# Last quad of the down projection by token halves, a stacked operand for the time steps, and a later sum of squares in a hybrid decoder layer on one Trainium2 core

## What is computed

```python
def rmsnorm(x, g):
    y = x * lax.rsqrt(jnp.mean(x * x, axis=-1, keepdims=True) + EPS)
    return y * g
...
dt = softplus(h @ w_in[:, dt_columns] + ssm_dt_bias)      # 16 heads
h_t = exp(dt_t * A) * h_{t-1} + dt_t * x_t * B_t^T ;  y_t = h_t @ C_t + D * x_t
ssm = rmsnorm(y * silu(z), ssm_norm_g) @ ssm_w_out
...
x3 = x2 + ffn @ ffn_w_down
y  = rmsnorm(x3, final_norm_g)
```

## Time and profile before

| | |
|---|---|
| median of 3 runs | 1029.4 us (1029.18 to 1032.2) |
| profiled execution | 1031.21 us, of it 1029.4 us span |
| TensorE matmul busy | 1002.2 us (97%), 7994 instructions |
| VectorE busy | 623.4 us (61%) |
| ScalarE busy | 381.2 us (37%) |
| GpSimd busy | 282.0 us (27%) |
| granted TensorE clock, mean | 0.988 of full |

### The profile page before, as it was taken

How to read it: one execution, slowest core, us unless ns; L and a number is a source line. 1 busy time by engine, 2 the same in 40 slices (tenths; PEclk the granted TensorE clock), 3 DMA queues, 4 the chain that set the end, 5 groups by cost and what they waited for, 6 DMA issues and landing times.

```text
span 1029.4 us, 19474 instructions
## 1 busy us (share of the span) xinstructions
PE 1002.2 (97%) x7994; PEld 980.2 (95%) x7994; DVE 623.4 (61%) x970; ACT 381.2 (37%) x544; POOL 282.0 (27%) x212
## 2 busy tenths in 40 slices
PE   5999999999999999999999999999999999999996
PEld 5999989989998999989999999999999999999996
DVE  4799879975547788796533335555540036666453
ACT  4322337653631665525222334433321122322210
POOL 3200000000030001452344334444434454444350
PEclk9999989999999999999999999999999999999997
DMA  7423227323322323415272222323223332321222
GB/s 237 147 83 99 65 62 63 66 63 92 89 73 62 104 83 117 171 41 185 82 248 85 83 86 80 93 92 99 64 62 93 100 110 89 99 66 53 76 59 87
DMA packets 42605, 97.96 MB, mean 95 GB/s; under 512 B 14640, under 2 KB 15536, under 8 KB 42544
## 3 DMA queue, kind: packets, MB, share of 16 engines
q1 hardware_dynamic: 42544, 97.10, 31.8%
HBM read 89.15 MB, written 7.93 MB: 94 GB/s over the span
## 4 chain that ended last, share of the span: by engine, by line
PE 86%; DVE 11%; issue 1%; POOL 1%; ACT 1%; DMA 0%; SPq 0%; DVEq 0%
PE accs L382 79%; DVE temps L1480 2%; DVE ca L1417 2%; DVE w_split L330 1%; PE misc L950 1%; PE misc L1112 1%; PE misc L956 1%; DVE part L444 1%; PE misc L1077 1%; PE misc L963 1%; PE misc L1128 1%; POOL w_split L330 1%; PE misc L1117 1%; PE misc L1096 1%; DVE xbc L2078 0%
## 5 line engine op out<-in xcount | busy, mean ns | idle before, releaser
L382 PE MATMUL accs<-h_split,w_split 128*128 128x272 f32 x4992 | 637.1, 289 | 4.6 <-POOL h_split L580 2.9
L382 PEld LDWEIGHTS accs<-h_split,w_split 128*128 128x128 f32 x4992 | 628.9, 189 | 10.2 <-issue 4.4
L330 POOL TENSOR_TENSOR w_split<-w_raw,w_split 128x1024 fp32r<-128x1024 f32 (+2 forms) x112 | 252.6, 2263 | 445.1 <-ACT w_split L325 422.3
L382 PE MATMUL accs<-branch,w_split 128*128 128x272 f32 x2208 | 284.8, 290 | 0.0
L382 PEld LDWEIGHTS accs<-branch,w_split 128*128 128x128 f32 x2208 | 280.2, 189 | 3.0 <-issue 2.8
L325 ACT ACTIVATE w_split<-w_raw 128x1024 fp32r<-128x1024 f32 (+3 forms) x168 | 160.0, 962 | 238.4 <-PE accs L382 238.2
L1417 DVE SCALAR_TENSOR_TENSOR ca<-part,params,ca 128x512 f32<-128x512 f32 x120 | 83.7, 749 | 0.4
L330 DVE TENSOR_TENSOR w_split<-w_raw,w_split 128x1024 fp32r<-128x1024 f32 (+1 forms) x56 | 62.1, 1109 | 29.0 <-ACT w_split L325 28.8
L2066 DVE TENSOR_TENSOR xbc<-accs,xbc 128x544 f32<-128x544 f32 x16 | 11.6, 725 | 95.6 <-PE accs L382 95.6
L2043 DVE TENSOR_TENSOR temps<-temps,mixed 128x512 f32<-128x512 f32 x22 | 40.7, 1850 | 26.5 <-ACT temps L920 26.5
L768 ACT ACTIVATE temps<-accs,params 128x544 f32<-128x544 f32 x24 | 17.2, 715 | 93.1 <-PE accs L382 93.1
(11 more groups left out here) (253 smaller groups left out, 710.8 us busy)
## 6 DMA issues: line engine op xcount, KB each, us to landing
w_raw<-in_ffn_w_up SPq DMA_DIRECT2D x44, 512.0 KB, 3.6
w_raw<-in_w_in_main SPq DMA_DIRECT2D x28, 512.0 KB, 3.6
w_raw<-in_w_gate SPq DMA_DIRECT2D x24, 512.0 KB, 3.7
w_raw<-in_ffn_w_down SPq DMA_DIRECT2D x16, 384.0 KB, 3.0
w_raw<-in_ffn_w_down SPq DMA_DIRECT2D x16, 320.0 KB, 2.9
xbc<-in_x SPq DMA_DIRECT2D x16, 272.0 KB, 5.7
w_raw<-in_w_in_z SPq DMA_DIRECT2D x8, 512.0 KB, 3.5
w_raw<-in_ssm_w_out SPq DMA_DIRECT2D x8, 512.0 KB, 3.6
```

The costliest lines, as they stand in the source:

```text
L330: e.tensor_tensor(w_split[:, s, 1, 0:n], w_raw[:, s, 0:n], w_split[:, s, 0, 0:n].bitcast(F32), ALU.subtract).then_inc(w_lo[s], 1)
L382: mm = pe.matmul(accs[:, a, half, 0:HALF], w_split[:, s, wp, k * P:(k + 1) * P], rhs(s, k, xp, half), start=(first and k == 0 and n == 0), ...
```

## The change

Three edits in the work and one in bookkeeping.

1. **End.** D2's last quad runs all four slots for the left 272 tokens and then all four for the right ones. VectorE adds, squares and sums each half of blocks 6 and 7 by itself; each half has its own `token_sum`, root, reciprocal and `spread_rms` of three columns. The left half's `token_sum` stands inside the right half's stream before slot 1, its `spread_rms` in slot 2 at k-tile 1. The eight blocks are scaled and stored by halves (16 stores of 128 x 272).
2. **Time steps.** High and low weight parts lie side by side as 32 weight columns, so that one matmul over 272 columns makes both products: 32 matmuls. Five fp32 matmuls against a matrix `fold_dt` (32 x 16) add the two parts and turn them; `fold_dt` is one more small load on SyncE's queue. ScalarE copies 272 and 272 columns from 32 partitions.
3. **Sum of squares of the gated SSD.** `token_sum` moves from k = 2 to k = 4 of slot 1, `spread_rms` from k = 7 of slot 1 to k = 0 of slot 2. `new_state(3)` moves ahead of `y_times_z(6)`.
4. Five semaphores of cleared buffers become one that counts.

```diff
+            sp.dma_start(fold_dt[:, :], ins["fold_dt"]).then_inc(sem("small_landed"), 16)
...
-            for j in range(KD):
-                sp.wait_ge(sem("y_done"), j + 1)
-                sp.dma_start(outs["y"][:, j], xbc[:, j]).then_inc(sem("stored_y"), 16)
+            for n, (half, j) in enumerate(halves_out):
+                sp.wait_ge(sem("y_done"), n + 1)
+                sp.dma_start(outs["y"][:, j, tokens(half)], xbc[:, j, tokens(half)]).then_inc(sem("stored_y"), 16)
...
-                    act.activation(dt_rows[:, 0:SEQ], misc[0:HEADS, 2], ACT.Copy)
-                    act.activation(dt_rows[:, SEQ:TOK], misc[0:HEADS, 1, 0:SMP], ACT.Copy).then_inc(sem("dt_rows"), 1)
+                    act.activation(dt_rows[:, 0:HALF], misc[0:2 * HEADS, 2, 0:HALF], ACT.Copy)
+                    act.activation(dt_rows[:, HALF:TOK], misc[0:2 * HEADS, 1, 0:HALF], ACT.Copy).then_inc(sem("dt_rows"), 1)
...
-            act_phase(act, "D2", lambda i, s: None)
+            p = ph["D2"]
+            loop(act, 0, p.quads - 1, lambda i: act_quad(act, p, i, (p, i + 1), lambda i, s: None))
             sqrt_table()
-            root("nf", D)
+            for half in range(2):
+                c = slice(3 * half, 3 * half + 3)
+                act.wait_ge(sem("rms_sum"), nth("nf") + half)
+                act.activation(rms[:, 0, c], misc[:, 3, c], ACT.Sqrt, bias=eps[:, 0:1], scale=1.0 / D)\
+                    .then_inc(sem("rms_root"), 1)
...
-                    pe.transpose(misc[:, 2, c * HEADS:(c + 1) * HEADS], dt_rows[:, c * CH:(c + 1) * CH],
-                                 ident[0:HEADS, 0:HEADS])
+                    pe.matmul(misc[:, 2, c * HEADS:(c + 1) * HEADS], dt_rows[:, c * CH:(c + 1) * CH], fold_dt[:, :],
+                              start=True, stop=True)
...
-                    for n, (wp, xp) in enumerate(((0, 0), (0, 1), (1, 0))):
-                        for bank, cols in ((2, slice(0, SEQ)), (1, slice(SEQ, TOK))):
-                            mm = pe.matmul(misc[0:HEADS, bank, 0:cols.stop - cols.start], w_dt_split[:, wp, k],
-                                           h_split[:, k, xp, cols],
-                                           start=(k == 0 and n == 0), stop=(k == KD - 1 and n == 2))
+                    for half in range(2):
+                        for xp in range(2):
+                            mm = pe.matmul(misc[0:2 * HEADS, 2 - half, 0:HALF],
+                                           w_dt_split[:, k].rearrange("p q h -> p (q h)"), h_rhs(0, k, xp, half),
+                                           start=(k == 0 and xp == 0), stop=(k == KD - 1 and xp == 1))
...
-                if (s, k) == (1, 2):
+                if (s, k) == (1, 4):
                     pe.wait_ge(sem("yz_sq"), 1)
                     token_sum(T(2))
-                if (s, k) == (1, 7):
+                if (s, k) == (2, 0):
                     spread_rms("ns")
...
+            def last_halves():
+
+                i = p.quads - 1
+                for half in range(2):
+                    for s in range(SLOTS):
+                        a = p.acc(s)
+                        if half == 0:
+                            pe.wait_ge(w_lo[s], i + (p.quad0 + 1))
+                            if s % 2 == 0:
+                                pe.wait_ge(acc_free[a], p.pair(i, s))
+                        for k in range(p.kb[s]):
+                            if (half, s, k) == (1, 1, 0):
+                                pe.wait_ge(sem("x3_sq"), 1)
+                                token_sum(T(5), range(3))
+                            if (half, s, k) == (1, 2, 1):
+                                spread_rms("nf", range(3))
+                            for n, (wp, xp) in enumerate(((0, 0), (0, 1), (1, 0))):
+                                mm = pe.matmul(accs[:, a, half, 0:HALF], w_split[:, s, wp, k * P:(k + 1) * P],
+                                               rhs(s, k, xp, half), start=(s % 2 == 0 and k == 0 and n == 0),
+                                               stop=(s % 2 == 1 and k == p.kb[s] - 1 and n == 2))
+                        if s % 2:
+                            mm.then_inc(sem("last_half"), 1)
+            last_halves()
             keep_warm(WARM[3])
-            pe.wait_ge(sem("x3_sq"), 1)
-            token_sum(T(5))
+            pe.wait_ge(sem("x3_sq"), 2)
+            token_sum(T(5), range(3, 6))
             keep_warm(WARM[1])
-            spread_rms("nf")
+            spread_rms("nf", range(3, 6), 1)
...
             for k in range(KD):
+                if k == 6:
+                    new_state(3)
                 y_times_z(k)
...
                 if k == 6:
-                    for q in (3, 4, 5):
+                    for q in (4, 5):
                         new_state(q)
...
-            down("D2", True)
-            rstd("nf")
-            for j in range(KD):
-                dve.scalar_tensor_tensor(out=halves(xbc[:, j]), in0=halves(xbc[:, j]), scalar=param("final_g", j),
-                                         in1=stat, op0=ALU.mult, op1=ALU.mult).then_inc(sem("y_done"), 1)
+            down("D2", True, KD - 2)
+            def last_block(half, j):
+                a, own = j % 2, xbc[:, j, tokens(half)]
+                dve.wait_ge(sem("last_half"), 2 * half + a + 1)
+                link(dve.tensor_tensor(own, accs[:, a, half, 0:HALF], own, ALU.add))
+                link(dve.tensor_tensor(T(4)[:, tokens(half)], own, own, ALU.mult))
+                sums = T(5)[:, tokens(half)]
+                if j < KD - 1:
+                    link(dve.tensor_tensor(sums, sums, T(4)[:, tokens(half)], ALU.add))
+                else:
+                    dve.tensor_tensor(sums, sums, T(4)[:, tokens(half)], ALU.add).then_inc(sem("x3_sq"), 1)
+            def inverse_half(half):
+                c = slice(3 * half, 3 * half + 3)
+                dve.wait_ge(sem("rms_root"), nth("nf") + half)
+                dve.reciprocal(rms[:, 1, c], rms[:, 0, c]).then_inc(sem("rms_inverse"), 1)
+            def scaled_half(half, js):
+                dve.wait_ge(sem("rms_spread"), nth("nf") + half)
+                for j in js:
+                    own = xbc[:, j, tokens(half)]
+                    dve.scalar_tensor_tensor(out=own, in0=own, scalar=param("final_g", j), in1=misc[:, half, 0:HALF],
+                                             op0=ALU.mult, op1=ALU.mult).then_inc(sem("y_done"), 1)
+            last_block(0, KD - 2)
+            last_block(0, KD - 1)
+            inverse_half(0)
+            last_block(1, KD - 2)
+            scaled_half(0, range(6))
+            last_block(1, KD - 1)
+            scaled_half(0, range(6, KD))
+            inverse_half(1)
+            scaled_half(1, range(KD))
```

More of the change, by code:

```diff
@@ L37 @@
 EPS = 1e-6
+EPS_SET, ROWS_ZERO, ZEROS_A, ZEROS_X, ZEROS_F = range(1, 6)
 SLOTS = 4
@@ L169, in build @@
         fold = sb("fold", [P, SMP])
+        fold_dt = sb("fold_dt", [2 * HEADS, HEADS])
         head_of = sb("head_of", [64, HEADS], F32R)
@@ L239, in head_decay @@
             return T(2 + h % 4, SEQ)
-        dt_rows = temps[0:HEADS, 5, 0:TOK]
+        dt_rows = temps[0:2 * HEADS, 5, 0:TOK]
         def norm_block(j):
@@ L435, in build @@
         last_decay = small[:, 0:2].rearrange("p q n -> p (q n)")[:, 0:HEADS * NB].rearrange("p (h b) -> p h b", h=HEADS)
+        halves_out = [(0, j) for j in range(KD)] + [(1, j) for j in range(KD)]
         def sum_bank(q):
@@ L534, in _ @@
                 sp.wait_ge(sem(f"h0_stored{b}"), 16)
-            sp.wait_ge(sem("stored_y"), 16 * KD)
+            sp.wait_ge(sem("stored_y"), 16 * 2 * KD)
         @block.gpsimd
@@ L649, in root @@
                     .then_inc(sem("rms_root"), 1)
-            act.wait_ge(sem("eps_set"), 1)
+            act.wait_ge(sem("cleared"), EPS_SET)
             sqrt_table()
@@ L715, in evac_x @@
                 if b < 2:
-                    act.wait_ge(sem("zeros_x"), 1)
+                    act.wait_ge(sem("cleared"), ZEROS_X)
                     act.wait_ge(sem("gl_sq"), 1)
@@ L945, in _, with token_sum @@
             groups = [(h * HALF + o, n) for h in range(2) for o, n in ((0, P), (P, P), (HALF - P, HALF - 2 * P))]
-            def token_sum(src):
-                for c, (t0, _) in enumerate(groups):
+            def token_sum(src, cs=range(6)):
+                for c in cs:
+                    t0 = groups[c][0]
                     mm = pe.matmul(misc[:, 3, c:c + 1], src[:, t0:t0 + P], ones[:, 0:1], start=True, stop=True)
@@ L956, in keep_warm, with spread_rms @@
                     pe.matmul(misc[:, 2, 0:P], ones, ident, start=True, stop=True)
-            def spread_rms(name):
-                pe.wait_ge(sem("rms_inverse"), nth(name))
-                for c, (t0, n) in enumerate(groups):
+            def spread_rms(name, cs=range(6), more=0):
+                pe.wait_ge(sem("rms_inverse"), nth(name) + more)
+                for c in cs:
+                    t0, n = groups[c]
                     at = t0 % HALF + P - n
```

(13 more changed lines are left out.)

30 lines of the change are left out of this document (16 added, 14 removed).

## The result

The changed kernel takes 1023.63 us (median of 6 runs, 1021.67 to 1025.52) against 1029.5 us (6 runs, 1028.59 to 1032.2): the ratio is 0.9939, with a 95% interval of 0.9922 to 0.9956. It is faster, by 0.6%. The forecast of 1021.8 us was 1.8 us too low, inside the range's upper end of 1025.8. The profiled execution took 1023.7 us, of it a span of 1021.9 us, 7.5 us under the profiled execution before.

What follows compares the result with a forecast made beforehand. TensorE's own work was taken as 86% of the chain of waits, VectorE's as 11%. Time steps -2.1, Z to G1 -1.0 and end -4.5 sum to -7.6 us, from 1029.4 to 1021.8 us; range 1018.5 to 1025.8.

Steps and rivals of the forecast that it cites:

- Time steps: In X: 32 matmuls replace 48, the wait before the third mix covers the added products; -2.1 us.
- the row of the fold: In X: the profile's fold, 0.23 us per product, used to price the five fp32 products at 1.2 us.
- such a fall at 207 us: Third mix: a 1.72 us wait in 207 to 209 us left the clock at 1.00, so whether it falls is luck.
- Z and G1: Step from Z to G1: waits of 2.28 us become one of 1.3 us for `ssm_lo`; -1.0 us.
- I keep the loss: G1: the clock falls after the new wait as before, costing 1.55 us of dense matmuls; change 0.
- The end: Last quad and tail by token halves: -0.6 - 0.75 - 2.05 - 2.45 + 1.35 = -4.5 us.
- The full clock of the last spread: Tail: the three-column spread takes 0.7 us at full clock instead of 2.74; -2.05 us, or -1.35 at half clock.
- The sum: Whole kernel: -2.1 - 1.0 - 4.5 = -7.6 us; profiled span from 1029.4 to 1021.8 us.
- by the same difference 1021.8 us: Whole kernel: the profiled execution's saving applied to the median of runs, from 1029.4 to 1021.8 us.
- slow stores: Rival, end: half-block stores do not go twice as fast, +2.5 us, 1024.3 us; chance 0.11.
- stall in the last quad: Rival, last quad: TensorE waits for weights from GpSimd's late splits; slower, 1033.6 us; chance 0.04.
- loss on VectorE in X: Rival, X: VectorE's stretch does not move, the third mix's wait grows; -5.5 us, 1023.9 us; chance 0.12.

Runs made afterwards that it cites:

- The single parts: Kernel before with only the fourth state addition moved ahead, 1032.09 us, and with only the sum of squares and its spread moved later, 1030.02 us; one run each.
- later sum alone: Kernel before with the sum of squares at k-tile 4 and its spread at the head of slot 2, fourth state addition unmoved: 1030.02 us, one run.
- state addition back: Changed kernel with the fourth state addition back behind block 6's product, sum of squares still at k-tile 4: 1021.87 us, ratio to the kernel before 0.9920.
- fillers in G1: Changed kernel with 5 filler matmuls in front of the 1.6 us wait in slot 1 of G1: 1022.52 us, ratio 0.9922.
- best: Changed kernel, fourth state addition back, fillers: 6 ahead of the 129 us wait, 5 more after the first norm's spread, 10 after A's first k-tile: 1018.95 us, ratio 0.9887.
- time steps alone: Kernel before with only the time-step edit and the split-weight layout it needs: 1026.45 us against 1030.71, ratio 0.9962.
- end alone: Kernel before with only the end edit (last quad by token halves, two final norms, 16 stores): 1026.5 us against 1030.71, ratio 0.9963.
- Z and G1 alone: Kernel before with only the later sum of squares and spread and the earlier fourth state addition: 1030.01 us against 1030.71, ratio 0.9996.
- turned twice: Changed kernel with 10 instead of 5 products that turn the time steps: 1024.7 us, one run.
- whole stores: Changed kernel with 8 stores of whole blocks instead of 16 of halves: 1027.2 us, ratio to the kernel before 0.9969.
- no filler after the end: Changed kernel without the 8 filler matmuls after the last dense matmul: 1025.03 us, ratio to the kernel before 0.9939.
- fillers in X: Changed kernel with 6 filler matmuls in front of the wait for the gMLP's sum of squares at 129 us: 1018.93 us, ratio 0.9899.
- state addition alone: Kernel before with only the fourth state addition moved ahead of block 6's product: 1032.09 us, one run.
- the first experiments: Kernel before with one edit each: time steps 1026.45 us, Z and G1 1030.01 us, end 1026.5 us, against 1030.71 us (20 runs).

## Why the prediction was right, and where it was not

Point by point, against its own terms:

- **Time steps:** -2.1 was forecast, -2.3 came at the third mix (2.19 from the matmuls themselves, 0.1 from what stands behind them). VectorE's stretch moved with TensorE, as the argument had it. The wait fell to 0.94, 1.0 was forecast. The five products took 1.15 us, 1.2 by the row of the fold. The Trainium skill (TensorE: Matmul & The Clock Gate, Terms) has transpose mode four times faster for FP32, and the prediction's estimate from that was 1.7 us. The trace does not agree: five transposes of 16 partitions took 0.38 us before (165.80 to 166.18), so the five products, of 32 partitions, took three times as long and not four. The term can be worth more than its sum: the clock fell behind the long wait in three of five profiles, where a fall cost 0.93 us, and behind the shorter one in none of eight. The prediction named such a fall at 207 us, but priced it only in G1.
- **Z and G1:** -1.0 forecast, -0.85 came (32.68 to 31.83). The mechanism was right: the wait went and came back as one of 1.64 us (1.3 forecast) that names `ssm_lo`. "The new wait has the same length and the same six products behind it, so I keep the loss" held in the profile of the changed kernel, and not as a rule. With the wait of 1.6 us the clock stayed down for longer in two of the six profiles (33.4 us for the step) and did not fall in one (30.28). The edit alone measured as nothing; in its profile the step's gain was there and the fall at the third mix took it. The single parts show a better choice that the prediction did not weigh.
- **The end:** -4.5 forecast, -4.35 came. The tail shrank by 5.7 us (5.8 forecast) and the inner sum and spread put 1.3 us into the stream (1.35 forecast). The sum behind the filler started at T + 1.78 (1.98 forecast), half a block cost VectorE 0.42 us (0.37), and scaling and stores took 6.2 us (5.95), with SyncE's issue at 0.44 us. The full clock of the last spread was forecast, but 1.2 of its 2.05 us was luck of the profile before: with the old tail the spread ran in 1.51 us in three of five profiles and in 2.74 in two.
- **The sum** was -7.6 against the profiled execution, and that execution's successor is 7.5 lower. That the three parts fill the 7.5 so well is in part luck. Ahead of the edits the clock differed too: up to the sum over channels in VU the profile after is 1.57 us later (110.45 against 108.88), from there to the time steps 1.55 us shorter (29.75 against 31.30), and both reach them at 140.2. The step that was off is the last one, "by the same difference 1021.8 us": the profiled execution before (1031.21) was 1.7 us above the median of its six runs, so a difference taken from it need not hold for the median. If the median run had its last spread at full clock, the same terms give -7.6 + 1.2 = -6.4, from the median 1023.0 us; no profile of a median run shows whether it had.
- **The rivals:** slow stores did not come; whole blocks, the other way, cost 1.9 us. Here what counts is when the bytes may leave. The Trainium skill (DMA: Bandwidth & Descriptors, Bandwidth) has DMAs batched into large ones. The rates of this case point the same way (381 to 390 GB/s in whole blocks, 270 to 282 in halves, where the issues set a part of the pace), and the kernel's time points the other way. No stall in the last quad, no loss on VectorE in X.

What stays open: the three edits alone gain 4.3, 0.7 and 4.2 us by their medians, 9.2 together, and the changed kernel gains 5.9 over its own runs before. The kernel before itself had a median of 1030.71 us beside the single edits and 1029.5 beside the changed kernel, which is 1.2 us of the gap. The intervals are 1.7 to 3.5 us wide each, and the clock's losses need not add up; no run here divides the rest between the two.

## What to carry to other kernels

A wait that is removed from the list is worth only what the engine behind it can give: ask which chain of the other engine ends next, and test each half of an edit by itself. Where TensorE's clock can fall, two short waits can be better than one long wait of the same sum, and fillers in front of a long wait can pay though they leave the wait's end where it is. Before a difference is taken from one profiled execution, set that execution beside the median of its runs and take out what differs by luck.

## What the runs showed of the hardware

TensorE's clock, by the granted clock in the windows. After the wait in slot 1 of G1 with six one-column products behind it, with the step's length from the sums 3 to 5 to slot 3:

| wait, us (profiles) | kernels | clock | step, us |
|---|---|---|---|
| 0.25 to 0.49 (4) | later sum alone, state addition back, fillers in G1, best | up in all | 30.27 to 30.28 |
| 1.16 (3) | before, time steps alone, end alone | down in all, 0.81 over 471 to 480 us | 32.68 to 32.71 |
| 1.56 to 1.64 (6) | changed, Z and G1 alone, turned twice, whole stores, no filler after the end, fillers in X | down in five, up in one | 31.80 to 31.84, 33.37 to 33.39, 30.28 |
| 2.51 (1) | state addition alone | down, 0.64 over 471 to 480 us | 34.24 |

The three kernels of the second row have the sum at k = 2, and the wait of 1.12 us in Z besides. One fall of the shorter kind costs 1.55 us of dense stream, one of the longer 3.1.

The wait at 129 us (1.76 us, six one-column products behind it) shows the same sizes. From the sum over channels in VU to the time steps it is 28.2 us in the two profiles with fillers, where the clock stays up, 29.74 to 29.76 in five and 31.30 to 31.34 in seven; the clock fell in all twelve without fillers. The wait was the same in these twelve, so its length does not decide how long the clock stays down. The longer fall stands in the seven profiles whose sum behind the wait starts at 129.2 to 130.5 us, the shorter in the five at 130.8 to 131.6: when the wait comes goes with it here; why is not shown. At the third mix a fall behind 1.7 us cost 0.93 us only; a later wait of 0.35 us for VectorE went with it, which is a part of the difference.

The times of single runs come in steps too: the kernel before has runs at a mean clock of 0.991 at 1028.8 to 1029.7 us and runs at 0.986 or 0.988 at 1030.6 to 1032.0 us, in the 20 runs beside the first experiments. With fp32 fillers of 128 columns in front of it, a wait of 0.43 us (at 129 us, two profiles) or 0.49 us (in G1, one) left the clock up. Fillers are no guarantee: at the old end of the kernel eight of them stand ahead of a wait of 0.62 us, and the clock was down at the last spread in two of five profiles. Behind 2.3 us of fp32 products with 16 columns (the turning products made twice) it fell in the one profile.
